# Decoder layer with an HGRN2 mixer: sample tokens' states updated from v rows brought to all partitions through memory, instead of from outer products on TensorE

## The reference, cut to what matters

```python
proj = rmsnorm(h) @ w_in                       # columns: q | f | v | g | u
q = silu(q_raw) * 128 ** -0.5
fg = lb + (1 - lb) * sigmoid(f_raw)            # one forget factor per head and key index d
k = 1 - fg
# per sample sequence b and head h, with S0 = state_hgrn[b, h], a 128 x 128 matrix [d, v]:
S_new[d, v] = fg[d] * S0[d, v] + k[d] * v[v]   # returned as new_hgrn_sample
o[v]        = sum_d q[d] * S_new[d, v]
```

## Time and profile before

| | |
|---|---|
| runs | 1171.48, 1170.54, 1169.45 us; median 1170.54 |
| profiled execution | 1170.06 us; its span in the trace 1168.2 us |
| busy, TensorE | 1156.9 us of the span (99%), granted clock 0.998 |
| busy, VectorE / ScalarE / GpSimd | 1006.4 / 565.1 / 55.5 us |
| DMA | 201 GB/s over the span |

### The profile page before, as it was taken

One profiled execution on the slowest core, in us unless ns is written; L12 is line 12 of the kernel. 1 busy time (PEld: TensorE's weight loads), 2 busy tenths in 40 slices (PEclk: granted clock), 3 DMA queues, 4 the chain that ended last, 5 costly groups with the idle time before them and its releaser, 6 DMA issues.

```text
span 1168.2 us, 31003 instructions
## 1 busy us (share of the span) xinstructions
PE 1156.9 (99%) x12469; PEld 1037.3 (89%) x12469; DVE 1006.4 (86%) x1575; ACT 565.1 (48%) x810; POOL 55.5 (5%) x80
## 2 busy tenths in 40 slices
PE   8999999999999999999999999999999999999997
PEld 7888888888888899899998999989989999999886
DVE  6778799778867898998989989888899999998687
ACT  6545645654546644444444444444444444444443
POOL 2122310100000200000000000000000000000000
PEclk9999999999999999999999999999999999999999
DMA  8767876766566566666666666666666666667561
GB/s 253 238 200 207 237 217 192 232 190 190 181 211 199 180 216 199 195 194 204 215 200 195 194 202 215 203 193 194 201 199 215 202 199 207 206 199 242 163 190 75
DMA packets 193385, 234.92 MB, mean 201 GB/s; under 512 B 8010, under 2 KB 153777, under 8 KB 193040
## 3 DMA queue, kind: packets, MB, share of 16 engines
q1 hardware_dynamic: 187984, 221.08, 60.4%
q0 software_dynamic: 3968, 11.89, 3.6%
q10 hardware_dynamic: 1360, 0.92, 0.3%
HBM read 226.89 MB, written 7.43 MB: 201 GB/s over the span
## 4 chain that ended last, share of the span: by engine, by line
PE 93%; DVE 4%; ACT 1%; issue 1%; DMA 0%; DVEq 0%; ACTq 0%
PE acc L2322 13%; PE acc L1924 10%; PE acc L1926 10%; PE acc L1928 10%; PE acc L2363 7%; PE acc L2325 6%; PE acc L2324 6%; PE acc L2303 6%; PE acc L2305 6%; PE wrk L2303 4%; PE wrk L2305 4%; PE acc L2365 2%; PE acc L2366 2%; DVE hl L977 2%; PE wrk L2081 1%
## 5 line engine op out<-in xcount | busy, mean ns | idle before, releaser
L977 DVE SCALAR_TENSOR_TENSOR hl<-raw,hl 128x1024 f16<-128x1024 f32 x414 | 493.7, 1220 | 51.7 <-ACT hl L610 49.0
L610 ACT ACTIVATE hl<-raw 128x1024 f16<-128x1024 f32 x414 | 420.3, 1051 | 168.8 <-DMA raw<-in_w_down_dram 88.0
L2322 PE MATMUL acc<-nrm,hl 128*128 128x264 f16 x1344 | 274.8, 276 | 0.3 <-DVE tg L1481 0.3
L1926 PE MATMUL acc<-nrm,hl 128*128 128x264 f16 x920 | 253.9, 276 | 0.0
L1928 PE MATMUL acc<-nrm,hl 128*128 128x264 f16 x920 | 253.9, 276 | 0.0
L1924 PE MATMUL acc<-nrm,hl 128*128 128x264 f16 x920 | 253.9, 276 | 0.0
L2324 PE MATMUL acc<-nrm,hl 128*128 128x264 f16 x672 | 185.5, 276 | 0.0
L2325 PE MATMUL acc<-nrm,hl 128*128 128x264 f16 x672 | 185.5, 276 | 0.0
L2322 PEld LDWEIGHTS acc<-nrm,hl 128*128 128x128 f16 x1344 | 129.0, 98 | 18.1 <-DVE tg L1481 0.6
L2363 PE MATMUL acc<-big,hl 128*128 128x264 f16 x704 | 130.2, 276 | 0.0
L1924 PEld LDWEIGHTS acc<-nrm,hl 128*128 128x128 f16 x920 | 90.2, 98 | 13.2 <-issue 0.3
(11 more groups left out here) (492 smaller groups left out, 2241.9 us busy)
## 6 DMA issues: line engine op xcount, KB each, us to landing
raw<-in_w_gate_up_dram SPq DMA_DIRECT2D x168, 512.0 KB, 4.6
raw<-in_w_down_dram SPq DMA_DIRECT2D x88, 512.0 KB, 4.0
raw<-in_w_in_dram SPq DMA_DIRECT2D x80, 512.0 KB, 4.7
raw<-in_w_out_dram SPq DMA_DIRECT2D x32, 512.0 KB, 5.0
raw<-in_w_ple_gate_dram SPq DMA_DIRECT2D x32, 512.0 KB, 5.0
state<-in_state_hgrn_dram POOLq DMA_DIRECT2D x8, 512.0 KB, 6.6
out_new_hgrn_sample_dram<-state POOLq DMA_DIRECT2D x8, 512.0 KB, 5.3
raw<-in_w_gate_up_dram SPq DMA_DIRECT2D x16, 256.0 KB, 3.8
```

What stands on the lines that cost most here:

```text
L610: nc.scalar.activation(hi[:, st.hl_slot(j, half), :], raw[:, st.raw_slot(j), :], ACT.Copy, scale=WSCALE).then_inc(hi_done, 1)
L977: stt(lo[:, st.hl_slot(j, half), :], raw[:, st.raw_slot(j), :], WSCALE, hi[:, st.hl_slot(j, half), :], ALU.mult, ALU.subtract).then_inc(lo ...
L1926: mm(out, wh, x_lo[:, kt, :], start=False, stop=False)
L2322: mm(out, wh, n_hi[:, kt, :], start=jj == 0 and kk == 0, stop=False, skip_group_check=bool(up))
```

## The change

The fp16 halves of k and v, the transposes of `kv_wide`, the outer products and the copy to `kv_smp` go. For each quad of heads, VectorE packs the 4 x 8 v vectors (128x32), TensorE transposes them in fp32 at b = 25 and 49 (one job), ScalarE copies the 32 rows to SBUF and writes them by a DMA to a tensor in memory (`v_rows`, 16 KB). One block later ScalarE waits for that write and issues loads that bring each head's 8 rows (4 KB) to all 128 partitions (`v_bc`, 512 KB in SBUF, two buffers). At r = 1 and 3 of a pair ScalarE multiplies one head's states by f, 8 instructions of 128x128 in place with a per-partition scale; at r = 2 and 4 VectorE adds k * v, 8 instructions for one head. The store of each head waits for that head alone. `SAMPLE_AT` becomes 27, 38, 51, 58.

```diff
-SAMPLE_AT = (26, 38, 50, 58)
+SAMPLE_AT = (27, 38, 51, 58)
+ROWS_AT = (25, 49)
...
+    if _b in ROWS_AT:
+        JOBS += [(f"vs_{ROWS_AT.index(_b)}", "act")]
     for _p in range(PAIRS):
         _r = _b - SAMPLE_AT[_p]
-        if _r == 0:
-            JOBS += [(f"kv_{_p}", "act")]
-        elif _r in (2, 4):
-            JOBS += [(f"ou_{_p}_{_r - 2 + j}", "dve") for j in range(2)]
-        elif _r == 10:
+        if _r == 10:
             JOBS += [(f"os_{_p}", "dve")]
...
-            nc.gpsimd.memset(scores[:, 0:2], 0.0)
-            nc.gpsimd.memset(kv_wide[0], 0.0)
-            for n in range(2):
-                last = nc.gpsimd.memset(win[n][:, :, 0:WPAD], 0.0)
-            last.then_inc(zero_ready, 1)
+            nc.gpsimd.memset(scores[:, 0:2], 0.0).then_inc(zero_ready, 1)
...
                 for h in (2 * p, 2 * p + 1):
-                    pool.wait_ge(drained["dve"], drain_of(f"ou_{p}_3")[1])
+                    pool.wait_ge(state_new, h + 1)
...
                 if p == 1:
-                    pool.wait_ge(job_done, job_value("sb"))
-                    nc.gpsimd.memset(kv_wide[1], 0.0).then_inc(zero_ready, 1)
...
+            for n in range(2):
+                last = nc.gpsimd.memset(win[n][:, :, 0:WPAD], 0.0)
+            last.then_inc(zero_ready, 1)
...
+            def value_rows(c, r):
+                if r == 0:
+                    wait_job(f"vs_{c}")
+                    nc.scalar.activation(vs_tok, wrk[0:4 * NSAMP, JOB[f"vs_{c}"] % JOB_BANKS, 0:P], ACT.Copy)\
+                        .then_inc(drained["act"], 1)
+                    act.wait_ge(drained["act"], drain_of(f"vs_{c}")[1])
+                    act.dma_start(v_rows[c], vs_tok).then_inc(vs_out, 16)
+                elif r == 1:
+                    act.wait_ge(vs_out, 16 * (c + 1))
+                    for h in range(2):
+                        rows_to_all(4 * c + h)
+            def rows_to_all(h):
+                n = NSAMP * P
+                src = bass.AP(v_rows.tensor, v_rows.offset + h * n, [[0, P], [1, n]])
+                act.dma_start(v_bc[h % 2].rearrange("p b v -> p (b v)"), src).then_inc(v_bc_in[h % 2], 16)
...
             def sample_part(p, r):
-                if r == 0:
...
+                if r in (1, 3):
+                    h = 2 * p + r // 2
+                    act.wait_ge(state_in[h % 2], 16 * (p + 1))
+                    act.wait_ge(acc_free, TPG * (3 * (p // 2) + 3))
+                    for b in range(NSAMP):
+                        s = state[:, h % 2, b, :]
+                        last = nc.scalar.activation(s, s, ACT.Copy, scale=f_all[:, h, SEQ + b:SEQ + b + 1])
+                    last.then_inc(state_kept, 1)
                 elif r in (5, 6):
...
+                    if p % 2 == 0:
+                        rows_to_all(h + 2)
...
+                for c in range(QUADS):
+                    value_rows(c, b - ROWS_AT[c])
...
-            def pair_states(p, bs):
...
+            def new_states(h):
+                dve.wait_ge(v_bc_in[h % 2], 16 * (h // 2 + 1))
+                dve.wait_ge(state_kept, h + 1)
+                for b in range(NSAMP):
+                    s = state[:, h % 2, b, :]
+                    last = stt(s, v_bc[h % 2][:, b, :], k_all[:, h, SEQ + b:SEQ + b + 1], s, ALU.mult, ALU.add)
+                last.then_inc(state_new, 1)
             def sample_halves(c):
-                hs, wide = slice(4 * c, 4 * c + 4), kv_wide[c]
+                hs = slice(4 * c, 4 * c + 4)
                 dve.wait_ge(acc_free, TPG * (3 * c + 3))
-                dve.wait_ge(zero_ready, c + 1)
+                nc.vector.tensor_copy(vs_pack.rearrange("p (h b) -> p h b", h=4), v_all[:, hs, SEQ:TOK]).then_inc(vs_packed, 1)
...
                 if r in (2, 4):
-                    pair_states(p, (r - 2, r - 1))
+                    new_states(2 * p + r // 2 - 1)
...
+            def sample_values(c):
+                pe.wait_ge(vs_packed, c + 1)
+                out = job(f"vs_{c}")
+                nc.tensor.transpose(out[0:4 * NSAMP, 0:P], vs_pack, ident[:]).then_inc(job_done, 1)
+                yield
...
                 for c in range(QUADS):
                     yield from quad_jobs(c, b - QUAD_AT[c])
+                if b in ROWS_AT:
+                    yield from sample_values(ROWS_AT.index(b))
```

More of the change, by code:

```diff
@@ L309, in build @@
         sc16 = xe[:, 4160:5696].bitcast(F16).rearrange("p (n a h t) -> p n a h t", n=2, a=3, h=4)
-        kv_smp = xe[:, 0:512].bitcast(F16).rearrange("p (s h j d) -> p s h j d", s=2, h=2, j=2)
+        vs_tok, vs_pack = xe[0:4 * NSAMP, 0:P], xe[:, P:P + 4 * NSAMP]
+        v_bc = [xe[:, n:n + 1024].rearrange("p (b v) -> p b v", b=NSAMP) for n in (3136, 2048)]
+        v_rows = nc.dram_tensor("v_rows", (QUADS, 4 * NSAMP, P), F32, kind="Internal").ap()
         buf_tok = xe[0:NSAMP * POOL_BUF, 1024:2048]
@@ L315, in build @@
         u_last = xe[0:POOL_BUF + NSAMP, 3136:4160]
-        kv_wide = [xe[:, n:n + 1024].bitcast(F16).rearrange("p (s c r) -> p s c r", s=2, r=32) for n in (3136, 1024)]
         sb_sum = sb("sb_sum", [P, 8, NSAMP])
@@ L411, in build @@
         sf_out = sem("sf_out")
+        vs_out, v_bc_in = sem("vs_out"), [sem("v_bc_in0"), sem("v_bc_in1")]
+        state_kept, state_new = sem("state_kept"), sem("state_new")
         pool_ready, pd_hi_ready, pd_ready = sem("pool_ready"), sem("pd_hi_ready"), sem("pd_ready")
@@ L416, in build @@
         out_chain, ffn_chain, down_chain, gate_chain = (sem(n) for n in ("out_chain", "ffn_chain", "down_chain", "gate_chain"))
-        e_rstd, e_ready, osq_ready, kv4_ready, xn_bc, rs_final = sem("e_rstd"), sem("e_ready"), sem("osq_ready"), sem("kv4_ready"), sem("xn_bc"), sem("rs_final")
+        e_rstd, e_ready, osq_ready, vs_packed, xn_bc, rs_final = sem("e_rstd"), sem("e_ready"), sem("osq_ready"), sem("vs_packed"), sem("xn_bc"), sem("rs_final")
         y_scaled = sem("y_scaled")
@@ L760, in quad_part @@
                         .then_inc(sf_out, 16)
-            def sample_part(p, r):
-                if r == 0:
[L765 to L770, removed]
+            def value_rows(c, r):
[13 more added lines that the diff above has]
+                act.dma_start(v_bc[h % 2].rearrange("p b v -> p (b v)"), src).then_inc(v_bc_in[h % 2], 16)
+            def sample_part(p, r):
+                if r in (1, 3):
[6 more added lines that the diff above has]
+                    last.then_inc(state_kept, 1)
                 elif r in (5, 6):
                     h = 2 * p + r - 5
-                    act.wait_ge(drained["dve"], drain_of(f"ou_{p}_3")[1])
+                    act.wait_ge(state_new, h + 1)
                     if p:
@@ L1198, in sample_halves @@
                 stt(q16[:, hs, :, 1], q_s, Q_UP, q16[:, hs, :, 0], ALU.mult, ALU.subtract).then_inc(q16_ready, 1)
[L1199 to L1204, removed]
             def take_diagonal(c):
@@ L1293, in window @@
                 wait_job(f"ut_{g // 2}")
+                dve.wait_ge(zero_ready, 2)
                 dst = win[0]
@@ L2045, in prompt_v @@
                     yield
[L2047 to L2057, removed]
             def diagonal(c):
@@ L2156, in sample_jobs @@
             def sample_jobs(p, r):
[L2158 to L2163, removed]
+                if r == 10:
                     out = job(f"os_{p}")
```

## The result

The changed kernel takes 1175.41 us (median of 8 runs, 1174.35 to 1177.37), the kernel before, on the same chip in turn, 1170.89 (8 runs, 1169.45 to 1172.79): a ratio of 1.0042, 95% interval 1.0033 to 1.0051. It is 4.5 us slower. The forecast was 1172.8 within 1167 to 1177, "slower" at 42%. The profiled execution took 1177.37 us, the slowest of the eight and just past the stated range, with a span of 1175.3 against 1168.2 before: 7.1 us more, where the medians differ by 4.5.

What follows compares the result with a forecast made beforehand. TensorE, busy 99% of the span, was taken as the bound; -5.3 + 0.2 + 0.4 + 4.5 + 2.7 = +2.5 us on the profiled 1170.06 gave 1172.6, named as 1172.8, range 1167 to 1177.

Steps and rivals of the forecast that it cites:

- Small matmuls: TensorE drops 32 transposes (1.8 us) and 8 outer-product steps (3.5), together -5.3; two fp32 transposes add 0.2.
- Wait for the pack at block 25: TensorE reaches the v job at 94.1, VectorE's packed v is ready at 94.5: stall +0.4 us.
- Waits up to block 49: Late pack 1.4, TensorE earlier by 0.9, VectorE 2.2 late behind ScalarE's scaling at block 39: 4.5 us, partly at level jobs.
- ScalarE's eight scalings: Multiplying one head's states by f, eight instructions at 0.26 to 0.29 us each: 2.1 to 2.3, taken as 2.3 us.
- VectorE's products at no gain: VectorE's new-state products read SBUF only, yet were taken to save nothing against the old ones on PSUM (348 against 346 ns).
- Head 6's load and block 64: Load issued at 212.1, landing at 217.8, delays ScalarE and block 63's gates; TensorE stalls 2.7 us at block 64, bounds 0 to 5.
- Rival 3, memory traffic: Broadcast loads land late and weight blocks with them, holding VectorE's splits: sum +5.5, 1176 us, slower decisively; 10%.
- Hidden parts: ScalarE's wait for the v_rows write at blocks 26 and 50, at most 5 us, is covered; uncovered, each up to 3 us.
- Rival 1, waits covered: TensorE loses at most 0.5 us to waits and the rest of the 5.3 gain stays: 1165.8 us, faster; 22%.

Runs made afterwards that it cites:

- version with work in place of the wait: Changed kernel plus 40 additional 264-column matmuls on TensorE at the start of block 64, into a bank nobody reads: 1174.02 us, ratio 1.0035 to the kernel before.
- the version of the last experiment: Three such moves, but pair 1's scaling and new states also one block later, its halves as in the changed kernel: 1167.93 us, ratio 0.9981 to the kernel before.
- three such moves: Changed kernel with second v job at 50, first-head halves of pairs 0 to 2 a block earlier, last pair's scaling and new states a block later: 1169.59 us.

## Why the prediction was right and where it was not

Direction, sign of the sum and, for the median, the range held; the forecast lay 2.6 us below the measured median. Up to block 55 that was the working. Behind it the range held by its width: the stall at block 64 came near the upper bound of its term, a cost came on top that had no term, and the profiled execution, which the sum was worked out for, gained 7.1 us where the sum has 2.5. Step by step:

- *Small matmuls, -5.3 and +0.2.* Right. Blocks 23 to 39 lose 1.31 us where the terms give 1.25, and the kernel before with fewer of them has the pace (-1.9) that its steps and its one new wait give.
- *Wait for the pack at block 25, 0.4.* It is 0.2 and 0.17 for the refill (last section).
- *Waits up to block 49, 4.5.* Right: the view shows 1.9 + 1.8 = 3.7 in four waits, each with 0.17 behind it, together 4.4. Both causes were shown apart: the version without scaling removed the level scores' part, the later v job the other.
- *ScalarE's eight scalings, 2.3 us.* 145.17 to 147.52 is 2.35. *VectorE's products at no gain:* 348 ns for 64 of them against 346. The Trainium skill, "VectorE: DVE Perf Modes", section on the TRN2 errata, has 62 cycles less for an SBUF source than for PSUM; these rows don't bear that out.
- *Head 6's load and block 64, 2.7.* The chain was right to its parts, 11.0 us from scaling to gates included; its term was mis-sized. The load was taken to land 5.7 us after issue and took 7.6: 1.9. The issue came at 213.2 instead of 212.1, but 0.8 of that is TensorE's lag at block 55, which shifts both sides as the text said; 0.3 is left. These 2.2 are the difference between the term, 2.7, and what was lost, 4.8 with the refill. The wait was 4.6, near the upper bound of 5 that the text gave for "a landing 2 us later". In six traces of this placement the load landed after 5.3 to 7.6 us, so the same sum could as well have met a shorter stall.
- *What the sum had not:* TensorE's clock behind that wait, 2.8 us in this trace and 2.2 to 2.5 in four others with a wait of 4.5 or 4.6. This is the step that failed, one left out: a long wait was priced at its length alone. Had it been in, the sum would have been -5.1 + 0.4 + 4.5 + 4.8 + 0.5 (the end-state job, with its refill) + 2.8 = +7.9 for the trace's pace of +7.8.
- *Rival 3, memory traffic.* No. The broadcasts landed after 4.3 to 7.5 us, VectorE never waited for one, and leaving six out changed nothing.
- *Hidden parts.* ScalarE did wait 3.9 us for the write of `v_rows` at block 26, and in this trace that was hidden. In three of the eleven traces of versions with `v_rows` it was not quite: ScalarE's first split behind it came late (in the version with work in place of the wait at 104.24 instead of 102.47, since the write took longer and the issue of the two broadcasts 2.2 us instead of 0.8), VectorE's first gate product followed at 115.79 instead of 114.19, and TensorE waited 1.1, 0.8 and 0.4 us at block 32. The prediction had said that each such wait costs up to 3 us once its cover is gone.
- *Rival 1, waits covered.* Not by the kernel as it stood, but the version of the last experiment has part of it: with 2.5 us of waits left it is 1.8 us faster than before, where the rival had 4.7. The change was worth having; the four block numbers were not.

Open is why the plain runs of the changed kernel lie 1 to 2 us below its profiled ones, and why they scatter more (1173.3 to 1177.4). Three things that vary are in the traces: the landing of head 6's load, how much of the half clock falls on work (4.4 to 5.7 us of it), and the gate product at block 32. A plain run gives only its time and its mean granted clock, and these go together: the nine of thirteen runs with 0.994 to 0.996 took 1174.4 to 1177.4 us, the four with 0.997 or 0.998 took 1173.3 to 1174.9. Where in the run the clock fell they don't show. Not tried: the moves in the kernel before, which had no wait in this stretch for them to take away.

## What to carry to other kernels

Before an operation is moved to an engine that is half idle, ask what is queued behind it there: ScalarE had the time for eight scalings, but not at the block where VectorE had caught up with it, and not behind a load. Price a wait on TensorE at more than its length, and look at the granted clock after each one of several microseconds. And when a change takes work off the engine that bounds the kernel and still costs time, move its parts by a block before giving it up: here three such moves turned 4.5 us lost into 1.1 won.

## What the runs showed of the hardware that was not expected

- *The clock.* With waits of TensorE of 4.6, 4.5, 4.0 and 3.1 us the granted clock went to 0.50 and came back to 1.00 under full work; 4.4 to 5.9 us of work ran at 0.50 each time, so 2.2 to 2.9 us were lost on top of the wait. Behind waits of 2.3, 1.8 and 1.2 us past 60 us it stayed at 1.00. But the length of the wait isn't all: behind the same 1.27 us at 16 us it was 0.50 in two traces and 1.00 in eleven, at a cost of 1.5 us. With matmuls in place of the wait at block 64 it stayed up. The Trainium skill, "TensorE: Matmul & The Clock Gate", Part 1, has an idle level of 1.2 and a busy level of 2.4 GHz; the trace agrees.
- *Refill.* A wait costs more than the view shows. Before the level scores of block 47 the last matmul starts at 167.79, the next would be due 0.11 later at 167.90 and starts at 169.27: 1.37 us lost, 1.21 shown. The difference, 0.16 to 0.17, is the overlap of a matmul of 0.28 with its follower, and it stands at block 49 too (178.18 to 180.25, with 1.79 shown).

```profile
167.79 0.28 PE L1936 MATMUL acc<-nrm,hl 128*128 128x264 f16 x1
169.27 0.46 PE L2075 MATMUL wrk<-big,a 128*128 128x128 f32 x2 [1.21 <-ACT a L715]
```

- *Small steps.* A group of outer products over 4 rows costs TensorE 0.2 us as a group and 0.03 for each product.
- *GpSimd beside VectorE.* Two products of 1024 elements on GpSimd, 3.8 us, held a VectorE copy of 0.17 us until both had ended, while a split of 1024 elements kept its 1.26 us and the product beside it took 2.86 instead of 1.9.
